# The prologue of a two-block kernel taken by halves of the features: other order of the first weight loads, of the products behind scale and shift, and of the squares

## What is computed

```python
def rms_norm(x, g):
    y = xf * lax.rsqrt(jnp.mean(xf * xf, axis=-1, keepdims=True) + NORM_EPS)
    return (y * g.astype(jnp.float32)).astype(x.dtype)
def modulate(h, shift, scale):
    return h * (1.0 + scale) + shift
...
        mod_lat = (jax.nn.silu(c) @ w_mod[i] + b_mod[i])[:, None, :]
        mod_ctx = (jax.nn.silu(c_ctx) @ w_mod[i] + b_mod[i])[None, None, :]
        sh1, sc1, gt1, sh2, sc2, gt2 = jnp.split(mod_lat, N_MOD, axis=-1)
...
        hc = modulate(rms_norm(x_ctx, g_norm1[i]), csh1, csc1)
        h = modulate(rms_norm(x_lat, g_norm1[i]), sh1, sc1)
        u = h @ w_in
```

## Time and profile before

| | |
|---|---|
| time, median of 3 runs | 1700.58 us (1699.9 to 1702.26) |
| the profiled execution's own time | 1699.19 us |
| its span in the profile | 1697.4 us |
| PE busy | 1635.2 us, 96% of the span |
| DVE busy | 1149.6 us, 68% |
| ACT busy | 905.7 us, 53% |
| DMA share, slices 1 and 2 of 40 (0 to 85 us) | 9 and 5 tenths |

### The profile page before, as it was taken

One profiled execution on the slowest core, in us unless ns is written; L12 is line 12 of the kernel. 1 busy time (PEld: TensorE's weight loads), 2 busy tenths in 40 slices (PEclk: granted clock), 3 DMA queues, 4 the chain that ended last, 5 costly groups with the idle time before them and its releaser, 6 DMA issues.

```text
span 1697.4 us, 27974 instructions
## 1 busy us (share of the span) xinstructions
PE 1635.2 (96%) x10354; PEld 1403.1 (83%) x10354; DVE 1149.6 (68%) x2027; ACT 905.7 (53%) x1970; POOL 487.4 (29%) x936
## 2 busy tenths in 40 slices
PE   6998998999999999898999999999999999999998
PEld 3874586888888878577999887998899878999998
DVE  5668848877787347866555678785556787775555
ACT  4456725444353535756555666675444665764542
POOL 1432013000000022402000134277753161586720
PEclk9999999999999999999999999999999999999999
DMA  9524224555445222114545445442255445343450
GB/s 363 181 88 161 100 98 154 198 199 198 176 176 183 101 87 100 50 58 144 197 164 186 166 146 199 150 145 105 101 199 193 163 155 176 123 142 108 150 199 26
DMA packets 106393, 254.95 MB, mean 150 GB/s; under 512 B 2758, under 2 KB 9556, under 8 KB 103188
## 3 DMA queue, kind: packets, MB, share of 16 engines
q1 hardware_dynamic: 104890, 250.57, 41.4%
q0 software_dynamic: 1088, 2.56, 0.7%
q10 hardware_dynamic: 282, 0.04, 0.0%
HBM read 252.11 MB, written 1.05 MB: 149 GB/s over the span
## 4 chain that ended last, share of the span: by engine, by line
PE 51%; DVE 7%; ACT 3%; issue 1%; POOL 1%; DVEq 0%; ACTq 0%; POOLq 0%
PE ps L1367 12%; PE ps L1369 11%; PE ps L1368 11%; PE ps L1670 2%; PE ps L1671 2%; PE ps L1672 2%; DVE big_r L2522 2%; PE ps L1789 1%; PE ps L1792 1%; PE ps L1784 1%; ACT big_r L1901 1%; PE ps L1574 1%; DVE cst_r L2522 1%; DVE hT_r L2522 1%; PE ps L1606 1%
## 5 line engine op out<-in xcount | busy, mean ns | idle before, releaser
L1901 ACT ACTIVATE big_r<-ring 128x1024 fp32r<-128x1024 f32 (+2 forms) x224 | 234.9, 1049 | 373.1 <-PE ps L1369 352.9
L2522 DVE TENSOR_TENSOR big_r<-ring,big_r 128x1024 fp32r<-128x1024 f32 (+2 forms) x224 | 275.3, 1229 | 226.3 <-ACT big_r L1901 225.8
L1368 PE MATMUL ps<-big_r 128*128 128x256 f32 (+1 forms) x1064 | 352.9, 332 | 0.0
L1367 PE MATMUL ps<-hT_r,big_r 128*128 128x256 f32 (+1 forms) x768 | 245.7, 320 | 0.4 <-DVE big_r L2522 0.4
L1367 PE MATMUL ps<-big_r 128*128 128x256 f32 (+1 forms) x720 | 240.4, 334 | 3.6 <-DVE big_r L2522 1.7
L1369 PE MATMUL ps<-hT_r,big_r 128*128 128x256 f32 (+1 forms) x768 | 242.1, 315 | 0.0
L1369 PE MATMUL ps<-big_r 128*128 128x256 f32 (+1 forms) x720 | 237.9, 330 | 0.0
L1030 POOL TENSOR_TENSOR sq<-sq 128x256 f32<-128x256 f32 (+1 forms) x30 | 35.5, 1185 | 696.7 <-ACT sq L1858 695.1
L1368 PEld LDWEIGHTS ps<-big_r 128*128 128x128 f32 x1064 | 202.2, 190 | 18.3
L1367 PEld LDWEIGHTS ps<-hT_r,big_r 128*128 128x128 f32 x768 | 146.3, 190 | 9.6 <-issue 1.0
L1369 PEld LDWEIGHTS ps<-hT_r,big_r 128*128 128x128 f32 x768 | 146.2, 190 | 9.3
(11 more groups left out here) (432 smaller groups left out, 4264.2 us busy)
## 6 DMA issues: line engine op xcount, KB each, us to landing
ring<-in_w_in SPq DMA_DIRECT2D x42, 2048.0 KB, 7.9
ring<-in_w_mlp SPq DMA_DIRECT2D x32, 2048.0 KB, 8.7
ring<-in_w_mod SPq DMA_DIRECT2D x24, 2048.0 KB, 7.9
ring<-in_w_out SPq DMA_DIRECT2D x4, 2048.0 KB, 7.9
ring<-in_w_out_a SPq DMA_DIRECT2D x4, 2048.0 KB, 7.9
ring<-in_w_out_b SPq DMA_DIRECT2D x4, 2048.0 KB, 8.1
ring<-in_w_o SPq DMA_DIRECT2D x4, 2048.0 KB, 8.1
ring<-in_w_in SPq DMA_DIRECT2D x2, 1536.0 KB, 14.2
```

What stands on the lines that cost most here:

```text
L1367: mm(b[:, 0:T], w_hi[:, k, :], hi(k), start=(j == 0), stop=False)
L1368: mm(b[:, 0:T], w_hi[:, k, :], lo(k), start=False, stop=False)
L1901: act_fn(hi, raw, ACT.Copy).then_inc(hi_ready, 1)
L2522: V.tensor_tensor(lo, raw, hi.bitcast(F32), ALU.subtract).then_inc(lo_ready, 1)
```

## The change

Scale and shift are taken by halves of the features. `MOD_ORDER` goes from (2, 3, 0, 1) to (2, 0, 3, 1). mod 3 no longer passes through the ring but has a place of its own (`apart`, in `big`). The slots' order becomes mod 2, mod 0, win 0, mod 1, win 1, win 2; SP issues mod 2, mod 0, the first half of win 0 and mod 3 without a wait, then mod 1, then the second half of win 0. PE does all eight squares first. The products and columns of mod 3 and mod 1 move in between and behind the granules of win 0. `mod_scaled` is done by halves, and `shift_made`, which DVE calls between the chunks of `modulated_norm`, gets the later copies and sums.

```diff
-MOD_ORDER = (2, 3, 0, 1)
+MOD_ORDER = (2, 0, 3, 1)
+MOD_APART = 3
@@ plan_slots
-            slots += [("mod", i, n) for n in MOD_ORDER]
-        slots += [("win", i, n) for n in range(3)]
+            slots += [("mod", i, 2), ("mod", i, 0), ("win", i, 0), ("mod", i, 1), ("win", i, 1), ("win", i, 2)]
+        else:
+            slots += [("win", i, n) for n in range(3)]
@@ SP
                     sp.dma_start(ring[:, r, 0:k0, 0:src.shape[2]], src[:, 0:k0, :]).then_inc(head_landed, 16)
+                    sp.dma_start(apart, source(("mod", 0, MOD_APART))).then_inc(apart_landed, 16)
+                    rest = ring[:, r, k0:KC, 0:src.shape[2]], src[:, k0:KC, :], slot_landed[r]
+                    continue
                 sp.dma_start(ring[:, r, k0:KC, 0:src.shape[2]], src[:, k0:KC, :]).then_inc(slot_landed[r], 16)
+                if key == ("mod", 0, MOD_ORDER[-1]):
+                    sp.dma_start(rest[0], rest[1]).then_inc(rest[2], 16)
@@ PE
-                    mod_products(MOD_ORDER[0], range(KC))
-                    squares((tag, "n1"), cc("ones"), P, TOK, KC, lambda: mod_products(MOD_ORDER[1], range(KC)))
+                    squares((tag, "n1"), cc("ones"), P, TOK, KC)
@@
-                    mod_column(MOD_ORDER[0])
-                    mod_column(MOD_ORDER[1])
-                    for n in MOD_ORDER[2:]:
+                    for n in MOD_ORDER[:2]:
                         mod_products(n, range(KC))
                         mod_column(n)
@@ in_granule
+                            if i == 0 and (m, k) == (1, 1):
+                                mod_column(MOD_ORDER[2])
+                                mod_products(MOD_ORDER[3], range(KC))
                             pe.wait_ge(h_ready, h_before + 2 * m + k + 1)
@@
                 for m in range(4):
                     in_granule(0, m)
+                    if i == 0 and m == 0:
+                        mod_products(MOD_ORDER[2], range(KC))
+                    if i == 0 and m == 1:
+                        mod_column(MOD_ORDER[3])
@@ ACT, shift_hi
-                act.wait_ge((modA_made, modB_made)[which], i + 1)
+                if i or which:
+                    act.wait_ge((modA_made, modB_made)[which], i + 1)
...
                         if i == 0 and k % 4 == 0:
                             await_drained(act, (("a", 0), "modcol", k // 4))
-                        if k == 1:
-                            hi_to(w0 + 1)
                         if k in (2, 4):
+                            if i == 0 and k == 4:
+                                await_bank(act, (("a", 0), "modrow", MOD_APART))
@@
-                if i:
-                    hi_to(first_gran["win", i] + 1)
+                hi_to(first_gran["win", i] + 1)
@@ DVE, shift_made
-                if k in (0, 2):
-                    mod_row_copied(k // 2)
-                if k in (2, 4):
-                    n = k // 2 - 1
-                    mod_biased(0, 4 * n, 4 * n + 4, ("modcol", n))
+                if k == 1:
+                    mod_row_copied(MOD_ORDER[1])
+                if k == 2:
+                    mod_biased(0, 0, 4, ("modcol", 0))
+                if k == 4:
+                    mod_row_copied(MOD_ORDER[2])
+                    mod_biased(0, 12, 16, ("modcol", 3))
+                    mod_scaled(0, 8, RA["g1"], 0, modA_made, 4, KC)
+                if k == 5:
+                    mod_row_copied(MOD_ORDER[3])
+                if k == 6:
+                    mod_biased(0, 4, 8, ("modcol", 1))
@@ DVE, modulated_norm
-                    if shifts:
+                    if shifts and k not in (4, 5):
                         shift_made(k)
...
+                    if shifts and k in (4, 5):
+                        shift_made(k)
@@ DVE, before modulated_norm
-                    mod_row_copied(MOD_ORDER[0])
                     params_scaled(0)
                     angles_reduced(0)
                     V.tensor_copy(mask_bf[:, :], cc("mask")).then_inc(consts_made, 1)
-                    mod_row_copied(MOD_ORDER[1])
                     angles_reduced(1)
-                    for n in MOD_ORDER[:2]:
-                        mod_biased(0, 4 * n, 4 * n + 4, ("modcol", n))
-                    mod_scaled(0, 8, RA["g1"], 0, modA_made)
+                    mod_row_copied(MOD_ORDER[0])
+                    mod_biased(0, 8, 12, ("modcol", 2))
+                    mod_scaled(0, 8, RA["g1"], 0, modA_made, 0, 4)
```

More of the change, by code:

```diff
@@ L650, in program @@
         gain_rows = pb[:, 2, 0:2 * HD].rearrange("p (x d) -> p x d", x=2)
+        apart = big[:, 17 * TOK:17 * TOK + KC * SLOT].rearrange("p (k c) -> p k c", k=KC)
         mod_acc = pT[:, :, :, :].rearrange("p a b c -> p a (b c)").rearrange("p a (s c) -> p a s c", s=2)
@@ L664, in program @@
         head_landed = sem("head_landed")
+        apart_landed = sem("apart_landed")
         slot_landed = [sem(f"slot{r}_landed") for r in range(RING)]
@@ L1322, in mod_products @@
                 b = start_bank(key) if ks[0] == 0 else bank(key)
-                w = slot(("mod", 0, n))
+                if n == MOD_APART:
+                    pe.wait_ge(apart_landed, 16)
+                    w = apart
+                else:
+                    w = slot(("mod", 0, n))
                 for k in ks:
@@ L2465, in mod_biased, with mod_scaled @@
                 await_drained(dve, key)
-            def mod_scaled(i, scale_at, g_row, which, made):
-                g = prm[:, i, g_row:g_row + KC].unsqueeze(2).to_broadcast([P, KC, 2])
-                V.scalar_tensor_tensor(amod[:, i, which, :, :], mod[:, i, scale_at:scale_at + KC, :], 1.0, g, ALU.add,
-                                       ALU.mult).then_inc(made, 1)
-                dve.wait_ge(made, i + 1)
+            def mod_scaled(i, scale_at, g_row, which, made, k0=0, k1=KC):
+                g = prm[:, i, g_row + k0:g_row + k1].unsqueeze(2).to_broadcast([P, k1 - k0, 2])
+                ins = V.scalar_tensor_tensor(amod[:, i, which, k0:k1, :], mod[:, i, scale_at + k0:scale_at + k1, :], 1.0, g,
+                                             ALU.add, ALU.mult)
+                if k1 < KC:
+                    link(ins)
+                else:
+                    ins.then_inc(made, 1)
+                    dve.wait_ge(made, i + 1)
             def late_partial(j, q):
```

## The result

The changed kernel takes 1706.56 us (median of 6 runs, 1703.45 to 1707.88); the kernel before, on the same chip, 1700.24 (6 runs, 1697.65 to 1702.26). The ratio is 1.0033, 95% interval 1.0023 to 1.0044: slower by 0.33%, beyond the 0.2% that a measurement tells from no change. The profiled execution has a span of 1704.7 us against 1697.4, +7.3.

A forecast was written before the change was run, and what follows sets the result against it. PE, without idle time from 38.8 to 113 us, was taken to bound the kernel. -6.6 + 4.9 + 0.6 + 4.1 + 1.6 = +4.6 us on the median 1700.58 gave 1705.2; range 1699.5 to 1708.5, the forecast's own 1703.6 to 1706.5.

The forecast's parts named there:

- Part 1: PE's way to granule 0 of win 0: it starts at 32.3 us instead of 38.88, -6.6 us.
- Part 2: Behind granule 0's start: products and columns of mod 3 and mod 1 enter PE's stretch without idle time, +4.9 us.
- Part 3: New waits in win 0: +0.6 inside granule 1, +4.1 serial chain behind column 1, +1.6 half clock in granule 2.
- rival 2: The waits of part 3 are shorter or granule 0 starts earlier: 0 to +3.4 us, about 1702.5; chance 0.18.
- Sum: Whole kernel: the terms of parts 1 to 3 together, +4.6 us, or +3.8 if the clock holds in the gap.
- rival 1: Squares at the front: the early clock falls there all the same, +1.7 us, total +6.3, 1706.9 us; chance 0.10.
- rival 4: POOL's tables come later than their 3 us of cover: +3 more, about +7.5, 1708 us; chance 0.05.
- Rival 3: Wait behind column 1 covered: -1.7 us, 1698.9; with granule 0 at full clock too, -3.3, 1697.3; chance 0.09.

The follow-up runs named there:

- run 8: Changed kernel with the squares put back behind the products of mod 2, those of mod 0 between the halves: 1710.95 us, ratio 1.0063 to the kernel before.
- run 4: Changed kernel with the products of mod 3 moved back in front of granule 0: 1701.47 us, ratio 1.0004 to the kernel before.
- run 1: Changed kernel with ACT scaling granule 2's weights ahead of its wait for column 1: 1705.43 us, ratio 1.0031 to the kernel before.
- run 5: Changed kernel, mod 3's products before granule 0, columns and mod 1's products earlier, weight parts of granules 2 and 3 earlier: 1696.08 us, ratio 0.9975.
- run 7: Run 5 without its moves of the weight parts, PE's order the same: 1699.16 us, ratio 0.9989 to the kernel before.
- run 2: Changed kernel with POOL's loads waiting for the products of mod 0 instead of the last mod's: 1705.7 us, ratio 1.0027 to the kernel before.
- run 3: Kernel before with the squares ahead of both mod products and DVE's two bank copies behind the angle work: 1703.89 us, ratio 1.0019.

## Why the prediction was right

**Part 1, the way to granule 0.** Forecast 32.3 us, measured 32.03. Link by link: products of mod 2 at 20.86 (21.1), column 2 at 23.69 (23.8), column 0 at 28.06 (28.1). Run 8 shows that about half of the -6.85 us is the squares. Its granule 0 still begins 3.33 us earlier than 38.88; that this other part comes from waiting for two mods instead of four is argued from the order, no run takes it by itself.

**Part 2, +4.9 for what PE gets behind it.** Confirmed in size: products of 1.92 and 1.93 us, columns of 0.60 us. Run 4 moves one of these groups back and gets its 1.9 us and more.

**Part 3, +0.6, +4.1 and +1.6.** Waits of 0.54 and 4.13 us, and the clock at the half from 53 to 56. Runs 1, 5 and 7 take the long wait apart. Granules 2 and 3 take 10.75 us from 52.86 to 63.61, against 9.04 in run 5 at full clock, so the fall cost 1.7 (1.6). That it came out so close is in part luck: behind the same wait the two granules took 10.48 us in run 4, 10.64 in run 2 and 11.74 in run 1. Run 4 shows what the fall costs in granule 0, 1.9 us. The waits were as long as the order had let me add them up, so rival 2 (shorter waits) did not come.

**Sum.** +4.6 forecast, +4.96 at the start of win 1; granule 0, which takes 6.52 us instead of 6.16, is the largest piece that no term had. The measured difference of the medians, +6.3, is larger by 1.3, so the 1706.56 us lie just above the forecast's own 1703.6 to 1706.5, and nearer to rival 1's 1706.9 than to 1705.2; it is the trace, not the time, that decides between the two. What the sum lacked is a term for the stretch behind the prologue: I took the lag at win 1 as the lag of the end, and between 113 us and the end it grew from 4.95 to 7.3. The lower mean clock of the changed kernel's runs goes with that; that it is the cause is argued, not shown. As an estimate, with 0.97 us for 0.001, all six runs brought to a mean clock of 0.991 average 1705.0, the 58 runs before 1700.7, a difference of 4.3. Whether the changed start makes such pieces likelier or six runs happened to have more of them stays open: the five runs of run 8 have 0.9888, the five of run 1 0.9900, but the nine of run 2 0.9907, and run 3, with the old order, 0.9896. Part of the lower mean is the half clock in the prologue itself, which the forecast counts.

**POOL, and rival 4.** Its tables came 5.4 us later and not 10 (the first rotation at 70.72 against 65.36 in the earlier trace rows): between the first load's issue and the rotation there are 24.8 us instead of 29.8. Run 2 shows that they are covered in any case.

**The cold squares, rival 1.** They fell away: 16 matmuls in 7.10 us at a granted clock of 1.00. The Trainium skill, page "TensorE: Matmul & The Clock Gate", section "Part 4: PE-mode transpose", has transposes not count as work for the clock; this trace does not agree, the squares ran at full clock behind 6.3 us of nothing but transposes (6.75 to 13.08) and 0.75 us of idle time. **Rival 3** named the condition under which the change would gain, the covered wait and granule 0 at full clock, and put the floor at -3.3. Run 5 met that condition and went to -5.46 at win 1, since it also puts the products of mod 3 into the wait ahead of granule 0, where they cost nothing; the changed order does not.

## What to carry to other kernels

Splitting a chain in halves brings the first consumer forward, but each piece that is moved behind it lands on an engine that had no idle time there, and the second half brings its own serial chain through all engines; ask for each moved group whether the wait it leaves was not the better place for it (run 4), and place the producer half a stage ahead of its consumer (run 7). Keep out of that chain all that does not need its result (runs 1, 5 and 7). When an operation goes to the front, look at what was to be freed by the operation behind it, above all a slot that a load waits for (run 3). And look for work that PE can do in a wait: the waits of 3.3 to 4.2 us ahead of granules 0 and 2 here cost once in time and again in clock.

## What the runs showed of the hardware

The waits of PE ahead of a granule were paid twice. Granule 0 takes 6.5 us (32.03 to 38.55) in the changed kernel, behind a wait of 3.34 us, and in run 5 at full clock, its column included, 5.1 us (31.69 to 36.82). In all seven traces in which PE stood idle through the whole wait ahead of granule 0 (2.25 to 3.35 us), its first matmul took 0.71 or 0.72 us; in the three in which the products of mod 3 stand in that wait (runs 4, 5 and 7), 0.46, 0.46 and 0.63. Run 7 shows that such work does not always hold the clock up: there the products themselves ran at half clock, where it cost nothing.

A run's spread goes with its clock: 58 runs of one kernel lie between 1697.1 and 1703.3 us, and the mean granted clock between 0.989 and 0.994 goes with them (above), so for changes under 0.3% the mean clock of each run has to be read beside its time. One profiled execution is no measure of the whole either: that of run 5 is 5.46 us ahead at win 1, 5.72 at 622 us, 3.8 at the end of its span, with a mean clock of 0.993 like that of the kernel before, and its median is 5.35 lower.
